# Expert weights of a mixture-of-experts layer: gate and up side by side, one product of 512 columns, halves by row tiles

## What is computed

```
a = silu(xb @ w_gate_e[e]) * (xb @ w_up_e[e])     # xb: up to 32 tokens x 1024, weights 1024 x 256
y = a @ w_down_e[e]                               # 256 x 1024
```

## Time and profile before

| | |
|---|---|
| median of 3 runs | 786.74 us (785.53 to 787.59) |
| the profiled execution | 785.32 us |
| its span, first to last instruction | 783.5 us |
| mean granted clock of TensorE | 0.987 of 2.4 GHz |
| PE busy in the span | 736.3 us (94%) |
| DVE, ACT busy | 419.5 us (54%), 336.0 us (43%) |
| HBM read | 202.09 MB |
| the eight expert groups | about 280 to 472 us of the span |

### The profile page before, as it was taken

One profiled execution on the slowest core, in us unless ns is written; L12 is line 12 of the kernel. 1 busy time (PEld: TensorE's weight loads), 2 busy tenths in 40 slices (PEclk: granted clock), 3 DMA queues, 4 the chain that ended last, 5 costly groups with the idle time before them and its releaser, 6 DMA issues.

```text
span 783.5 us, 12531 instructions
## 1 busy us (share of the span) xinstructions
PE 736.3 (94%) x5178; PEld 608.7 (78%) x5178; DVE 419.5 (54%) x747; ACT 336.0 (43%) x603; POOL 30.0 (4%) x64
## 2 busy tenths in 40 slices
PE   9999999999999999998766879999999999999997
PEld 9898888888788876664544549999878888888885
DVE  4758646666667421110100207666658876777675
ACT  6766565455444421110110117566556534344433
POOL 0700000000000000000000001100002000000001
PEclk9999999999999999999988999999999999999999
DMA  8762566356968899999999998954433464454201
GB/s 313 282 256 95 197 246 250 140 175 238 373 241 326 340 380 421 420 421 419 422 420 420 421 417 340 409 210 150 152 118 143 148 246 161 175 202 172 97 1 54
DMA packets 31435, 203.97 MB, mean 260 GB/s; under 512 B 3729, under 2 KB 4113, under 8 KB 8849
## 3 DMA queue, kind: packets, MB, share of 16 engines
q1 hardware_dynamic: 31376, 203.15, 66.6%
HBM read 202.09 MB, written 1.05 MB: 259 GB/s over the span
## 4 chain that ended last, share of the span: by engine, by line
PE 76%; DMA 14%; ACT 3%; DVE 3%; SPq 2%; issue 1%; POOL 0%; DVEq 0%; POOLq 0%; ACTq 0%
PE ps L638 41%; PE ps L707 10%; DMA ext<-in_w_up_e 7%; PE ps L1001 5%; PE ps L710 5%; DMA raw<-in_w_gate_e 3%; PE ps L978 2%; SPq L486 2%; PE ps L1024 2%; DMA raw<-in_dense 2%; PE ps L1034 1%; DMA big<-in_rel_ext 1%; DVE wl L1697 1%; ACT wh L1286 1%; PE ps L1140 1%
## 5 line engine op out<-in xcount | busy, mean ns | idle before, releaser
L1697 DVE TENSOR_TENSOR wl<-raw,wh 128x1024 fp32r<-128x1024 f32 (+3 forms) x180 | 213.3, 1200 | 131.4 <-ACT wh L1286 130.2
L1286 ACT CAST wh<-raw 128x1024 fp32r<-128x1024 f32 (+3 forms) x180 | 182.4, 1031 | 63.7 <-PE ps L638 44.5
L638 PE MATMUL ps<-wh,fra 128*128 128x512 f32 (+3 forms) x668 | 189.3, 369 | 0.4 <-DVE gb L1911 0.4
L638 PEld LDWEIGHTS ps<-wh,fra 128*128 128x128 f32 x668 | 118.6, 189 | 19.3 <-issue 1.0
L638 PE MATMUL ps<-wl,fra 128*128 128x512 f32 (+3 forms) x334 | 121.4, 363 | 0.0
L707 PE MATMUL ps<-fra,wh 128*128 128x512 f32 x352 | 110.7, 396 | 0.7 <-DVE fra L1708 0.7
L710 PEld LDWEIGHTS ps<-fra,wl 128*128 128x128 f32 x352 | 66.1, 188 | 15.5
L638 PE MATMUL ps<-wh,frb 128*128 128x512 f32 x240 | 74.3, 391 | 0.0
L638 PE MATMUL ps<-fra,wh 128*128 128x256 f32 x400 | 73.8, 286 | 0.1
L638 PEld LDWEIGHTS ps<-wl,fra 128*128 128x128 f32 x334 | 62.9, 188 | 9.6
L710 PE MATMUL ps<-fra,wl 128*128 128x256 f32 x352 | 69.2, 278 | 0.0
(11 more groups left out here) (269 smaller groups left out, 938.9 us busy)
## 6 DMA issues: line engine op xcount, KB each, us to landing
raw<-in_dense SPq DMA_DIRECT2D x79, 1024.0 KB, 5.1
raw<-in_w_gate_e SPq DMA_DIRECT2D x28, 1024.0 KB, 24.1
ext<-in_w_up_e SPq DMA_DIRECT2D x24, 1024.0 KB, 26.1
ext<-in_w_down_e SPq DMA_DIRECT2D x16, 1024.0 KB, 24.3
big<-in_w_up_e SPq DMA_DIRECT2D x8, 1024.0 KB, 20.6
raw<-in_dense SPq DMA_DIRECT2D x10, 512.0 KB, 5.1
big<-in_w_gate_e SPq DMA_DIRECT2D x4, 1024.0 KB, 18.5
raw<-in_w_down_e SPq DMA_DIRECT2D x4, 1024.0 KB, 20.5
```

The lines of the kernel that those rows point to most:

```text
L638: t = e.matmul(o, a, w, start=first and n == 0, stop=final and n == 2, skip_group_check=not check)
L1286: e.copy(halves(q)[0], piece_view(q)).then_inc(*up("wh", q))
L1697: e.tensor_tensor(l, piece_view(q), h.bitcast(F), ALU.subtract).then_inc(*up("wl", q))
```

## The change

On the host, each expert's gate and up weights are put side by side: each row has 256 columns of gate and then 256 of up. The 1024 rows are divided into the upper ones (row tiles 0 to 3) and the lower ones (row tiles 4 to 7), and each of these is one contiguous transfer of 1 MB, 8 KB for each partition as before. `experts(g)` then has half as many matmuls, of 512 columns: the first half multiplies row tiles 0 to 3 with the four "upper" transfers, the second half row tiles 4 to 7 with the four "lower" ones, both into all of bank 0. The wait for "XE act" moves from the middle of the first half to the start of the second.

```diff
     for g in range(8):
-        for key, w in (("eg", "w_gate_e"), ("eu", "w_up_e"), ("ed", "w_down_e")):
+        for key, w in (("upper", a["in_e"][:, 0]), ("lower", a["in_e"][:, 1]), ("ed", a["w_down_e"][0])):
             for n in range(4 * g, 4 * g + 4):
-                wt.whole((key, n), a[w][0, n].reshape(P, -1, a[w].shape[-1]))
+                wt.whole((key, n), w[n].reshape(P, -1, 1024 if key == "ed" else 512))
...
-                src = {"eg": w_gate_e, "eu": w_up_e, "ed": w_down_e}[key][0, n_].rearrange("(p k) n -> p (k n)", p=P)
+                src = (w_down_e[0, n_].rearrange("(p k) n -> p (k n)", p=P) if key == "ed"
+                       else in_e[n_, 0 if key == "upper" else 1])
...
         def experts(g):
 
             enter(0, "expert a", g)
-            for half_, key in enumerate(("eg", "eu")):
+            for half_, key in enumerate(("upper", "lower")):
                 if half_ and g == 7:
                     warm(WARM[6], 3)
                 for n in range(4):
                     e.wait_ge(*landed(wt.raws[key, 4 * g + n]))
-                for kk in range(8):
-                    if half_ == 0 and kk % 4 == 0:
-                        e.wait_ge(*at(("XE dve", "XE act")[kk // 4], g))
+                e.wait_ge(*at(("XE dve", "XE act")[half_], g))
+                for kk in range(4):
+                    k = 4 * half_ + kk
                     for j in range(4):
-                        t = e.matmul(bank[0][32 * j:32 * j + 32, 256 * half_:256 * half_ + 256],
-                                     XE[:, kk, 32 * j:32 * j + 32], slot_view(wt.raws[key, 4 * g + j])[:, kk, :],
-                                     start=(kk == 0), stop=(kk == 7))
+                        t = e.matmul(bank[0][32 * j:32 * j + 32, :], XE[:, k, 32 * j:32 * j + 32],
+                                     slot_view(wt.raws[key, 4 * g + j])[:, kk, :], start=(k == 0), stop=(k == 7))
                 t.then_inc(*up("taken", key, g))
...
-            e.wait_ge(*at("taken", "eu", g))
+            e.wait_ge(*at("taken", "lower", g))
             e.activation(AE[z], bank[0][:, 0:256], ACT.Silu).then_inc(*up("expert silu", g))
...
+    rows = [a[n][0].reshape(32, P, 2, 4, 256).transpose(0, 2, 1, 3, 4) for n in ("w_gate_e", "w_up_e")]
+    a["in_e"] = np.concatenate(rows, axis=-1).reshape(32, 2, P, 2048)
```

More of the change, by code:

```diff
@@ L269, in beside, with build, program @@
             next(fill, None)
-def build(nc, wt, x, mem, positions, gate_b, w_gate_e, w_up_e, w_down_e, grow, w_route, b_route, rel_ext, cst, dense,
+def build(nc, wt, x, mem, positions, gate_b, w_gate_e, w_up_e, w_down_e, in_e, grow, w_route, b_route, rel_ext, cst, dense,
           out, force_general=False):
     with ExitStack() as ctx:
-        program(nc, ctx, x, mem, positions, gate_b, grow, w_route, b_route, rel_ext, cst, out, wt, dense, w_gate_e, w_up_e,
-                w_down_e, force_general)
-def program(nc, ctx, x, mem, positions, gate_b, grow, w_route, b_route, rel_ext, cst, out, wt, dense,
+        program(nc, ctx, x, mem, positions, gate_b, grow, w_route, b_route, rel_ext, cst, out, wt, dense, in_e,
+                w_gate_e, w_up_e, w_down_e, force_general)
+def program(nc, ctx, x, mem, positions, gate_b, grow, w_route, b_route, rel_ext, cst, out, wt, dense, in_e,
             w_gate_e, w_up_e, w_down_e, force_general):
@@ L429, in released @@
         key = wt.key[u]
-        return at("taken", key[0], key[1] // 4) if key[0] in ("eg", "eu", "ed") else at("taken", key)
+        return at("taken", key[0], key[1] // 4) if key[0] in ("upper", "lower", "ed") else at("taken", key)
     s_load = {n: sem("s_" + n) for n in ("ident", "mem0", "mem1", "mem2", "mem3", "cst", "x", "pos", "gate0", "gate1",
@@ L2453 @@
         "positions": np.ascontiguousarray(a["positions"].reshape(2, P).T), "gate_b": a["gate_b"],
-        "w_gate_e": a["w_gate_e"], "w_up_e": a["w_up_e"], "w_down_e": a["w_down_e"],
+        "w_gate_e": a["w_gate_e"], "w_up_e": a["w_up_e"], "w_down_e": a["w_down_e"], "in_e": a["in_e"],
         "grow": np.ascontiguousarray(np.stack([a["final_norm_g"], a["g_post_mix_2"][0], a["g_post_ffn_2"][0]])),
```

## The result

The changed kernel is slower: 790.04 us median (788.23 to 791.77, 14 runs) against 786.19 (785.03 to 789.30, 14 runs) for the kernel before, a ratio of 1.0047 (1.0036 to 1.0058). A second series gave 790.08 against 786.20, 1.0048 (1.0033 to 1.0063). One of its 17 executions of the kernel before took 1232.63 us, and its ratio leaves that one out. The forecast was 788.1 in a range of 785.2 to 790.3, with "no measurable change" as its likeliest case (0.71) and "slower" at 0.24. The range held, with 0.26 us to spare; the likeliest case didn't come, and what filled the range was none of the five cases on record.

A forecast was written before the change was run, and what follows sets the result against it. PE bounds the kernel, except the expert stage's end, bound by weight transfers. 785.32 - 0.05 (products) - 0.05 (transfers) + 0 (packets) + 0 (stall) + 1.5 (clock) = 786.7 profiled, 788.1 median; range 785.2 to 790.3.

The forecast's parts named there:

- the five cases on record: Whole-kernel outcomes, times and chances: 788.1 us (0.36), 790.1 (0.19), 786.6 (0.26), 785.4 (0.14) and 783.9 (0.05).
- The products: Expert-stage gate and up matmuls on PE: 512-column turns of 0.429 us, -0.05 us on the last half.
- The transfers: Expert weight stream: same pace and issue cost, start 0.05 us earlier after group 0's first half; -0.05 us.
- The code packets: PE's instruction fetches over the DMA engines: four packets fewer, 9 where 13 were; bounds 0 to -2.8 us, taken as 0.
- The forecast's price of 1.4 us for one packet: Weight stream: two down transfers landing 3.9 us apart instead of 2.5 were read as 1.4 us lost.
- The code stall: Group 7's first half, behind the branch: the 2.04 us stop for code would shift or vanish; taken as 0.
- 240 instructions behind the branch: One end for where code runs out: in group 7's first combine, where nothing covers it, +2.0 us.
- almost none: Other end for where code runs out: right behind group 7's branch, the stall staying covered by the weight wait.
- the stall gone, 0: Group 7, behind the branch: code has long arrived, so no stall there; the value taken, 0 us.
- the forecast's own sign: Group 7: the prediction is wrong in kind if the last half begins after 458.3.
- The clock: Group 7's last half: a 3.9 us idle before it lowers PE's clock; bounds 0 to +1.9 us, taken as +1.5.
- rival 2: Group 7: clock falls before the last half and code runs out in the combine, +2.0 us, 790.1; chance 0.19.

The follow-up runs named there:

- the second profile: The changed kernel, unaltered, profiled again because its first profile was of its slowest execution; profiled execution 790.38 us, series median 790.08 against 786.20, ratio 1.0048.
- the pair with 18 filler products: Changed kernel and kernel before, both without the general path's branch, group 7 filler raised from 6 to 18: 786.66 and 786.73 us against 785.64.
- pad 16: 16 unused tiny products added in group 5's wait, moving later code 64 instructions: changed kernel 787.50 us, ratio 1.0015; kernel before 787.99, 1.0016.
- pad 32: 32 unused tiny products added in group 5's wait, moving later code 128 instructions: changed kernel 787.91 us, ratio 1.0020; kernel before 790.32, 1.0049.

## Why the prediction was right or wrong

**The products: right.** From 280.44 to 283.47 there are 7 turns of 0.433 us, forecast 0.429; a last half takes 3.64 us (3.66 before). In kernels without a stall and with the clock up, the change is worth 0.1 us, which can't be told from nothing.

**The transfers: right but for their start.** The pace is near that of before (415 to 424 GB/s in the stretches shown, 419 to 427 in the earlier trace rows), the first issue after the hole, at 284.14, comes with the end of the first half, and the moved wait for "XE act" shows nowhere. What the forecast hadn't: the stream fills more slowly behind the hole. The first three issues take 2.95 us instead of 1.40, and from 276 to 290 the second profile moved 4.58 MB, the kernel before 5.07; from 290 to 455 it was 69.46 and 69.42 MB. The 0.49 MB are some 1.2 us at 420 GB/s, about the 1.1 us of the later landing. In the other changed kernels it was 4.44 to 4.80 MB, in the other kernels before 4.83 to 5.05. Why those issues take longer stays open.

**The code packets: right in number, small in effect.** 38 for 42, and 9 for 13 in the full stretch. I took 0 for the stream. The last landing was 1.1 us later in the changed kernel's second profile, and equal within 0.1 us in the pair with 18 filler products. Since the stream was short only behind the hole, the packets later in it aren't the cause. In the five profiles of changed kernels whose last half waits for its weights it starts at 457.21 to 458.85, in the three of kernels before at 458.12 to 458.73, so no effect of the packets on that landing can be told. The forecast's price of 1.4 us for one packet stays an inference from one pair of landings.

**The code stall: the step that failed.** I saw the stall and that its place would shift by half a packet, and gave the two ends as 240 instructions behind the branch (+2.0 us, uncovered) and "almost none", of which I wrote: "At almost none it stays covered". That was the wrong price. I took the 2.04 us for the length of the stall, wherever it comes. It is only what was left of some 6.2 us after PE had worked 57 records on. With the code missing at once, the whole 5.96 us stand idle, and the wait for the weights covers only a part. The place came out at this end, not at the 240 to which half a packet pointed, and neither of those two was my likeliest case (the stall gone, 0). The recorded counts pointed there themselves: 118 + 896 instructions less four packets of 247 leave 26, not 240. By the forecast's own sign, a last half that begins after 458.3, it was wrong in kind: that half began at 463.14.

**The clock: right in mechanism, wrong in place.** I put +1.5 us on the last half. In the changed kernel the long idle is the stall itself, so the clock falls ahead of the first half (6.04 us instead of 3.64) and is up again for the last. Where the stall is really gone, the term is what I said: 5.34 us with pad 16, 5.35 without the branch in the kernel before, 6.25 without it in the changed kernel and 6.58 with pad 32, each instead of 3.6, and medians 0.15% to 0.33% above the kernel before. Two of the four lie above my bound of +1.9 us (+2.6 and +2.9). Those kernels came to 787.5 to 788.5, where the forecast for that case was 788.1.

**The sum.** Forecast +1.4 us on the profiled execution, measured +5.1 between the profiles (785.32 to 790.38) and +3.9 between the medians. The profile's terms: a stall of 5.96 us ahead of the half instead of 2.04 in it, +3.9; the work of the first half, 6.04 us at the lower clock instead of 3.40 + 0.64, +2.0; a later start, 449.05 instead of 448.25 for the last transposes, +0.8, most of it from group 6's last half, which ran longer at the lower clock (6.02 us instead of 5.33); the idle of 1.50 us before the last half gone, -1.5. That is 5.2, against 5.0 measured at the start of the last half. That the median lies within 0.1 us of rival 2's 790.1 is luck. Rival 2 had the clock fall in the last half and a stall of 2.0 us in the combine; in this profile the last half takes 3.64 us and the combine has no such stall.

Shown by experiment: that the place of the code alone makes the loss (the kernel before with 32 tiny products loses it all, and the changed kernel with them has won back over half of it), that the rest goes with the clock in the last half (with more filler the medians are level with the kernel before), and that the change without both is neutral.

Argued from the counts: the kernel before with 128 instructions more and the changed kernel with 896 fewer lie 1024 instructions apart, about four packets of code, and have the same picture. The changed kernel with pad 32 lies 768, about three packets, before the kernel before, so its code would end at the same distance behind the branch, some 118 instructions. Its first half and the filler have only 64 + 24 records, and the last half begins at 458.85, long after the 6.2 us: so no gap shows, though the code is fetched as before. Not settled: why, at the place of the changed kernel, not even the first instruction behind the branch is at hand, and why the packet starts only 3.4 to 3.8 us after the last transposes.

The Trainium skill (Runtime: NRT & Kernel Launch, section Instruction fetch mechanics) says that a taken branch whose target isn't at hand forces a fetch before execution can go on. The trace agrees, with 5.95 and 5.96 us idle right behind the branch in two kernels and none in kernels without the branch. No run here shows which targets are at hand.

## What to carry to other kernels

Where a kernel has a branch, count the instructions that a change adds or takes ahead of it: here 896 fewer moved a stall from covered to uncovered and cost 0.5%, while the change itself was worth nothing. Before a stall is priced, ask what it is the rest of: it may end at a fixed time, and then what PE does until then decides. Filler products that keep the clock up are placed by time; when something ahead of them moves, they have to be placed anew, and a stall may be what holds them in the right place.

## What the runs showed that I had not expected

- Taking an unused branch out made the kernel before slower, 1.0033 (1.0019 to 1.0047). Of the 2.9 us between the spans of the two profiles, 1.7 are the last half at the lower clock.
- After the branch PE goes on 6.1 to 6.6 us after the last transposes, whether 0, 25 or 57 matmul records of the half were at hand.
- An idle of 2.42 us was followed by the lower clock in one profile (last half 5.26 us) and one of 1.86 us was not in another (3.64 us). Nor did a longer idle cost more: behind 3.27 us the half took 6.58 us, behind 4.52 us 5.35.
